# A four-part edit of a one-core mLSTM and mixture-of-experts step: stacked gate rows and an earlier gate product at the start, and the samples' tile ahead of the last prompt tile in the router

## The reference

```python
z = x @ w_in                       # q | k | v | o | 4+4 gate columns | pool input u | gate_A | gate_B
li, lf = gi + b_i, log_sigmoid(gf + b_f)
h, C, n, m = mlstm(q, k, v, li, lf, state_C, state_n, state_m)   # 4 heads x 256
y_a = (sigmoid(o) * head_norm(h)) @ w_proj_a
y_b = (causal_pool(u) @ w_pool * pool_scale) @ w_proj_b
x1 = layer_norm(ALPHA * x + (sigmoid(ga) * y_a + sigmoid(gb) * y_b) @ w_out)
probs = softmax(x1 @ w_router + b_router)          # 16 experts in 4 groups: best group, then its best two
y = layer_norm(ALPHA * x1 + sum over the two of weight * (silu(x1 @ w_gate[e]) * (x1 @ w_up[e])) @ w_down[e])
```

## Time and profile before

| what | value |
|---|---|
| median of 3 runs | 920.99 us |
| the runs | 921.68, 920.99, 919.57 us |
| the profiled execution | 921.98 us, of which its span is 920.6 us |
| mean granted clock of PE | 0.982 of full speed |
| busy: PE, DVE, ACT, POOL | 884.5, 587.3, 391.3, 87.2 us |

### The profile page before, as it was taken

One profiled execution on the slowest core, in us unless ns is written; L12 is line 12 of the kernel. 1 busy time (PEld: TensorE's weight loads), 2 busy tenths in 40 slices (PEclk: granted clock), 3 DMA queues, 4 the chain that ended last, 5 costly groups with the idle time before them and its releaser, 6 DMA issues.

```text
span 920.6 us, 14525 instructions
## 1 busy us (share of the span) xinstructions
PE 884.5 (96%) x6007; PEld 787.5 (86%) x6007; DVE 587.3 (64%) x825; ACT 391.3 (43%) x410; POOL 87.2 (9%) x88
## 2 busy tenths in 40 slices
PE   6999999999999999999999999999999999999975
PEld 6998888988889999999999996878888788778841
DVE  3735554745575371233233447899999999999946
ACT  4422132211432332322223104677777677777712
POOL 3000000000000001000101011301110011110043
PEclk8999999999999999999999998999999999999987
DMA  9784083483816042321322915799999999999657
GB/s 300 231 318 110 30 262 105 134 256 102 281 58 206 1 152 92 92 89 54 98 82 99 384 50 213 279 376 381 414 389 392 384 413 401 380 414 379 257 165 173
DMA packets 82212, 207.08 MB, mean 225 GB/s; under 512 B 4222, under 2 KB 57174, under 8 KB 69225
## 3 DMA queue, kind: packets, MB, share of 16 engines
q1 hardware_dynamic: 74184, 177.30, 53.4%
q0 software_dynamic: 7968, 28.93, 9.2%
HBM read 174.68 MB, written 33.76 MB: 226 GB/s over the span
## 4 chain that ended last, share of the span: by engine, by line
PE 74%; DVE 16%; issue 4%; ACT 3%; DMA 2%; POOL 0%; SPq 0%; DVEq 0%; ACTq 0%
PE psum L452 21%; PE psum L454 20%; PE psum L453 20%; DVE split_lo L1467 7%; PE psum L1908 2%; DVE last_lo L1467 2%; PE psum L1918 2%; PE psum L2131 2%; PE psum L1947 1%; DVE xgl L1627 1%; DMA xn<-in_x_prompt_dram 1%; ACT split_hi L1001 1%; PE psum L1933 1%; DVE hs L1636 1%; DVE gs L1633 1%
## 5 line engine op out<-in xcount | busy, mean ns | idle before, releaser
L452 PE MATMUL psum<-x_hi,split_lo 128*128 128x272 f32 x704 | 208.8, 297 | 2.0 <-DVE pbl L1430 1.2
L454 PE MATMUL psum<-x_hi,split_hi 128*128 128x272 f32 x704 | 202.3, 287 | 0.0
L453 PE MATMUL psum<-x_lo,split_hi 128*128 128x272 f32 x704 | 202.1, 287 | 0.0
L1467 DVE TENSOR_TENSOR split_lo<-raw,split_hi 128x2048 fp32r<-128x2048 f32 x72 | 163.3, 2286 | 7.9 <-ACT split_hi L1001 6.9
L1001 ACT CAST split_hi<-raw 128x2048 fp32r<-128x2048 f32 x72 | 137.5, 1912 | 44.1 <-PE psum L454 44.0
L447 DVE TENSOR_TENSOR split_lo<-raw,split_hi 128x2048 fp32r<-128x2048 f32 x35 | 80.0, 2289 | 115.0 <-ACT split_hi L428 114.9
L452 PEld LDWEIGHTS psum<-x_hi,split_lo 128*128 128x128 f32 x704 | 132.6, 188 | 7.3 <-issue 2.7
L453 PEld LDWEIGHTS psum<-x_lo,split_hi 128*128 128x128 f32 x704 | 132.7, 189 | 1.4 <-issue 1.0
L454 PEld LDWEIGHTS psum<-x_hi,split_hi 128*128 128x128 f32 x704 | 132.6, 188 | 0.0
L452 PE MATMUL psum<-split_hi,xgl 128*128 128x512 f32 x192 | 76.3, 398 | 1.3 <-DVE xgl L1627 1.2
L454 PE MATMUL psum<-split_hi,xgh 128*128 128x512 f32 x192 | 74.9, 390 | 0.0
(11 more groups left out here) (383 smaller groups left out, 1753.3 us busy)
## 6 DMA issues: line engine op xcount, KB each, us to landing
raw<-in_w_e_gate_dram SPq DMA_DIRECT2D x32, 1024.0 KB, 8.7
raw<-in_w_e_up_dram SPq DMA_DIRECT2D x32, 1024.0 KB, 8.6
raw<-in_w_e_down_dram SPq DMA_DIRECT2D x32, 1024.0 KB, 8.2
raw<-in_w_in_dram SPq DMA_DIRECT2D x26, 1024.0 KB, 5.6
cb<-in_state_C_dram SPq DMA_DIRECT2D x8, 1024.0 KB, 7.5
out_dram<-cb SPq DMA_DIRECT2D x8, 1024.0 KB, 5.8
y_slots<-ys POOLq DMA_DIRECT2D x15, 512.0 KB, 8.0
kv<-kv_rows SPq DMA_DIRECT2D x4, 1028.0 KB, 8.0
```

The source lines that it names most:

```text
L452: nc.tensor.matmul(out, a_lo, b_hi, start=first, stop=False)
L453: nc.tensor.matmul(out, a_hi, b_lo, start=False, stop=False)
L454: return nc.tensor.matmul(out, a_hi, b_hi, start=False, stop=last)
L1467: v.tensor_tensor(lo, raw2[:, n % MOE_SLOTS, :], hi.bitcast(F32), ALU.subtract).then_inc(w_lo, 1)
```

## The change

There are four parts.

1. **Stacked gate rows.** `g_r`, `em` and `w_r` become rows 0 to 3, 32 to 35 and 64 to 67 of one tile `turn3` of 68 partitions and 640 columns, cleared by DVE at the start. ACT copies the sample columns of all three in one instruction. PE makes 5 transposes of 68 rows in place of 15 of 4 rows. DVE picks the columns out of the wider result. `rep4` is gone.
2. **G earlier.** The samples' x tile is transposed into banks 2 and 3 and waits for `x_lo` of tile 1. G's first half (tokens 0 to 271) waits for three low parts, only its second for all five.
3. **POOL's small loads.** `nn` is issued after `nm_rows`; `gain`, `pscale`, `brt` and `wr` after `bm`.
4. **The router.** The order is 0, 1, 2, 4, 3. The last tile, now number 3, goes by columns: DVE adds columns 256 to 767 and takes the first half's statistics before the last 256 columns of the product exist; its last norm step, PE's transposes, ACT's copy and the logits are made in halves of 512 features, with four new semaphores. ACT makes only one expert split before this copy. SP loads `kv` ahead of tile 3's store alone.

```diff
+ROW_ORDER = (0, 1, 2, PT, 3)
...
+TURNED = 64 + H
...
+    g_r, em, w_r = (turn3[32 * q:32 * q + H, 0:N] for q in range(3))
...
-        return psum[:, 2 * (i % 4):2 * (i % 4) + 2, :]
+        b = i if i < PT else 1
+        return psum[:, 2 * b:2 * b + 2, :]
...
-            for i in range(NT):
-                if i == 3:
+            for n, i in enumerate(ROW_ORDER):
+                if n == NT - 1:
                     load_keys_values()
-                sp.wait_ge(x1_ok, i + 1)
+                sp.wait_ge(x1_ok, n + 1)
...
-            pl.dma_start(nn[:], state_n[0].rearrange("b h d -> (b h) d")).then_inc(nn_in, 16)
+        pl.wait_ge(cst_in, 16)
+
+
+        pl.wait_ge(nm_ok, 1)
+        pl.dma_start(nm_rows, nm[:]).then_inc(nm_out, 16)
+        pl.dma_start(nn[:], state_n[0].rearrange("b h d -> (b h) d")).then_inc(nn_in, 16)
+        pl.wait_ge(nm_out, 16)
+        pl.dma_start(bm[:].rearrange("p h n -> p (h n)"), nm_rows.rearrange("h n -> (h n)").partition_broadcast(P)
+                     ).then_inc(bm_in, 16)
+        with nc.allow_non_contiguous_dma(reason="small parameters"):
             pl.dma_start(gain[:], hn_gain[0].rearrange("h (c p) -> p (h c)", p=P)).then_inc(par_in, 16)
...
-        for q, row in enumerate((g_r, em, w_r)):
-            last = nc.scalar.copy(rep4[:, q, :].rearrange("p (g n) -> p g n", g=4),
-                                  row[:, SEQ:N].unsqueeze(1).to_broadcast([H, 4, NS]))
-        last.then_inc(em_ok, 1)
+        nc.scalar.copy(turn3[:, N:].rearrange("p (g n) -> p g n", g=3),
+                       turn3[:, SEQ:N].unsqueeze(1).to_broadcast([TURNED, 3, NS])).then_inc(em_ok, 1)
...
+            ac.wait_ge(xq_done, 1)
+            nc.scalar.copy(x1t[n % 2][:, 0:4, 0:r], src[:, 0:4, :]).then_inc(xq_ok, 1)
             ac.wait_ge(z_done, j + 1)
+            nc.scalar.copy(x1t[n % 2][:, 4:8, 0:r], src[:, 4:8, :]).then_inc(z_free[j % 2], 1)
...
-        for n in range(2):
-            expert_hi(n, z_done, Z["T", NT - 1] + 1)
+        expert_hi(0, z_done, Z["T", ROW_ORDER[-1]] + 1)
         evac_x1t(NT - 1)
+        expert_hi(1, z_done, Z["T", ROW_ORDER[-1]] + 1)
...
+        v.memset(turn3[:], 0.0)
...
+            ve_.wait_ge(tq_done, 1)
+            step(v.scalar_tensor_tensor(x1[:, i, 256:768], x1[:, i, 256:768], ALPHA, rest[:, 0:512], ALU.mult, ALU.add))
+            v.bn_stats(lst[:, i, 0, :], x1[:, i, 0:512])
+            ve_.wait_ge(z_done, j + 1)
+            v.scalar_tensor_tensor(x1[:, i, 768:DM], x1[:, i, 768:DM], ALPHA, rest[:, 512:768], ALU.mult, ALU.add
+                                   ).then_inc(z_free[j % 2], 1)
+            z_evacuated(ve_, j)
+            step(v.bn_stats(lst[:, i, 1, :], x1[:, i, 512:DM]))
...
+            if n == NT - 1:
+                v.scalar_tensor_tensor(x1[:, i, 0:512], x1[:, i, 0:512], hrs[:, i:i + 1], lnb[:, 0:512], ALU.mult, ALU.add
+                                       ).then_inc(xh_ok, 1)
+                v.scalar_tensor_tensor(x1[:, i, 512:DM], x1[:, i, 512:DM], hrs[:, i:i + 1], lnb[:, 512:DM], ALU.mult,
+                                       ALU.add).then_inc(x1_ok, 1)
...
-            if i == 4:
-                pe.wait_ge(x_lo_ok, 1)
+            if i == PT:
+                pe.wait_ge(x_lo_ok, 2)
...
-        pe.wait_ge(x_lo_ok, NT)
+        pe.wait_ge(x_lo_ok, 3)
...
+            if a == 1:
+                pe.wait_ge(x_lo_ok, NT)
...
-        for q, row in enumerate((g_r, em, w_r)):
-            for i in range(NT):
-                at = (q * NT + i) * H
-                src = row[:, i * P:i * P + P] if i < PT else rep4[:, q, :]
-                last = nc.tensor.transpose(narrow(T_COL)[:, at:at + H], src, ident[0:H, 0:H])
+        for i in range(NT):
+            last = nc.tensor.transpose(narrow(T_COL)[:, 96 * i:96 * i + TURNED], turn3[:, i * P:i * P + P],
+                                       ident[0:TURNED, 0:TURNED])
```

More of the change, by code:

```diff
@@ L74, in _wide_order @@
     order += [("WO", 0)]
-    for i in range(NT):
-        order += [("T", i)] + ([("XT", i - 1)] if i else [])
-    order += [("XT", NT - 1)]
+    for n in range(NT):
+        order += [("T", ROW_ORDER[n])] + ([("XT", ROW_ORDER[n - 1])] if n else [])
+    order += [("XT", ROW_ORDER[-1])]
     return {unit: i for i, unit in enumerate(order)}
@@ L1491, in _, with last_rows @@
         ve_.wait_ge(ln_in, 32)
-        for i in range(NT):
+        def last_rows(i):
+            j = Z["T", i]
+            rest = wide(j).rearrange("p b n -> p (b n)")
+            ve_.wait_ge(tq_done, 1)
[6 more added lines that the diff above has]
+            step(v.bn_stats(lst[:, i, 1, :], x1[:, i, 512:DM]))
+            step(v.bn_aggr(hmv[:, i, :], lst[:, i].rearrange("p q s -> p (q s)")))
+            v.tensor_scalar(hve[:, i:i + 1], hmv[:, i, 1:2], EPS, None, ALU.add).then_inc(lv_ok, 1)
@@ L1503, in _ @@
-            last.then_inc(z_free[j % 2], 1)
-            z_evacuated(ve_, J_WO)
-            z_evacuated(ve_, j)
-            row_stats(i, lv_ok)
+            if n == NT - 1:
+                last_rows(i)
+            else:
+                ve_.wait_ge(z_done, j + 1)
+                if i < PT:
+                    last = v.scalar_tensor_tensor(x1[0:r, i, 256:DM], x1[0:r, i, 256:DM], ALPHA,
+                                                  wide(j).rearrange("p b n -> p (b n)")[0:r, 0:DM - 256], ALU.mult,
+                                                  ALU.add)
+                else:
+                    for q in range(4):
+                        cols = slice(256 * q, 256 * q + 256)
+                        last = v.scalar_tensor_tensor(x1[0:r, i, cols], x1[0:r, i, cols], ALPHA,
+                                                      wide(j)[q * NS:(q + 1) * NS, 0, 0:256], ALU.mult, ALU.add)
+                last.then_inc(z_free[j % 2], 1)
+                z_evacuated(ve_, J_WO)
+                z_evacuated(ve_, j)
+                row_stats(i, lv_ok)
@@ L2068, in rest_of_rows @@
                 last = out_rows(i, q, wide(j).rearrange("p b (q n) -> p (b q) n", q=2)[:, q - 1, :])
+                if i == ROW_ORDER[-1] and q == 2:
+                    last.then_inc(tq_done, 1)
             last.then_inc(z_done, 1)
@@ L2089, in x1_columns, with logits_in @@
             for k in range(KT):
+                if n == NT - 1 and k == 4:
+                    last.then_inc(xq_done, 1)
+                    pe.wait_ge(x1_ok, n + 1)
                 last = nc.tensor.transpose(out[:, k, 0:r], x1[0:r, i, whole(k)], ident[0:r, 0:r])
             last.then_inc(z_done, 1)
-        def logits_in(i):
+        def logits_in(n):
+            i = ROW_ORDER[n]
             r = ROWS[i]
-            z_evacuated(pe, Z["XT", i])
+            if n == NT - 1:
+                pe.wait_ge(xq_ok, 1)
+            else:
+                z_evacuated(pe, Z["XT", i])
             for k in range(KT):
-                last = mm(narrow(T_LOGIT)[0:r, i * NE:(i + 1) * NE], x1t[i % 2][:, k, 0:r], wr[:, k, :],
+                if n == NT - 1 and k == 4:
+                    z_evacuated(pe, Z["XT", i])
+                last = mm(narrow(T_LOGIT)[0:r, i * NE:(i + 1) * NE], x1t[n % 2][:, k, 0:r], wr[:, k, :],
                           start=k == 0, stop=k == KT - 1)
@@ L2103, in _ @@
         rest_of_rows(0)
-        for i in range(1, NT):
-            if i < PT:
-                rest_of_rows(i)
+        for n in range(1, NT):
+            if ROW_ORDER[n] < PT:
+                rest_of_rows(ROW_ORDER[n])
             else:
                 sample_rows_of_out()
-            if i >= 2:
-                logits_in(i - 2)
-            x1_columns(i - 1)
+            if n >= 2:
+                logits_in(n - 2)
+            x1_columns(n - 1)
         logits_in(NT - 2)
```

68 lines of the change are left out of this document (31 added, 37 removed).

## The result

The changed kernel took 915.28 us (median of four runs, 914.45 to 915.86) against 920.89 before (919.57 to 921.68): ratio 0.9942, 95% interval 0.9927 to 0.9957, a gain of 5.6 us. The forecast was 916.8, a gain of 4.2, within 913.8 to 919.3. The profiled execution took 915.86 us with a span of 913.7 us and a mean granted clock of 0.986 (before 921.98, 920.6 and 0.982).

A forecast was written before the change was run, and what follows sets the result against it. PE bounds the kernel, with 74% of what ended last (DVE 16%). Gains of 2.8 (G earlier), 0.4 (stacked rows), 0 (loads) and 1.0 (router) sum to 4.2 us: 920.99 to 916.8 us, range 913.8 to 919.3.

The forecast's parts named there:

- five of 68 rows lie between 0.34 and 0.68 us; I take 0.6: Gate rows' transposes after K: five stacked ones take 0.6 us against 1.02 for fifteen; gain 0.4 us, bounds 0.3 to 0.7.
- Rival B: Clock dip after K (1.7 us) goes; G at full clock gives 0.9, router 0.7 more: 913.5 us; chance 0.13.
- within 3.6 us of uninterrupted matmuls: At G: clock returns after 3.5 us, 16 slow matmuls, then 32 fast; G ends at 20.6, gain 2.8 us.
- upper bound of 3.7: At G: clock never low, G ends at 19.15, but Q waits for its chunk's low part until 19.71; gain 3.7 us.
- Nothing above depends on it: POOL's loads at the start: five fewer transfers can only bring x tiles and first chunks earlier; gain 0.
- the middle between 0 and 1.9: Router: gain between 0 and 1.9 us, depending on PE's clock at the last tile; 1.0 us taken.
- The sign that was named for a wrong forecast: Router: PE's clock low across the last tile's logits, 0.2 us a pass.
- rival A: Only the start pays: clock falls before the last tile's logits, or the store's landing takes the router's gain; 917.8 us; chance 0.2.
- the forecast's 575.5: Router's end: tile 3's store, issued at 565.4, lands at about 575.5 us if it ends with the queue's bytes.
- Rival D: Slower: tile 3's store lands late and delays POOL's first gather; at 20 us it costs 3.7, 924.7 us; chance 0.04.
- C: The start doesn't arrive: G's clock rises when it does now (gain 1.1), router gives nothing; 919.6 us; chance 0.10.
- E: Change doesn't do what it says: G starts with the gate weights' low part, at 13.01; later only if DVE's order delays it; no separate chance.

The follow-up runs named there:

- e5: Kernel before with part 1 alone (stacked gate rows): 918.96 us, ratio 0.9979.
- e3: Kernel before with part 2 alone (G's first half waits for three low parts): 917.96 us, ratio 0.9969.
- e7: Kernel before with 14 extra unused transposes on PE in its wait ahead of G, G's start condition unchanged: 918.30 us, ratio 0.9974.
- e6: Kernel before with parts 2 and 3, without the stacked rows: 916.99 us, ratio 0.9963.
- e1: Kernel before with part 4 alone (the router's order and the halves): 920.69 us, ratio 1.0004.
- e10: Changed kernel with 8 filler transposes on PE in the router (2, 3 and 3): 915.70 us, ratio 0.9946.
- e8: Changed kernel with 20 filler transposes on PE in the router (8, 6 and 6): 915.06 us, ratio 0.9938.
- e12: Changed kernel with the 20 router fillers of e8 and 10 more in PE's wait behind the twelfth expert's second product: 913.67 us, ratio 0.9929.
- e4: Kernel before with part 3 alone (POOL's small loads later): 920.48 us, ratio 0.9993.

## Why the prediction was right, and where it was not

**The sum** of 4.2 us was 1.4 short of 5.6. The interval of the measured gain reaches from 4.0 to 6.7 us, so the total alone would not fault it; the parts do. The mechanism, an earlier G and nothing that waits in its place, was right; three terms were mis-sized. That the sum is as near as it is owes something to luck, since part 4's missing 1.0 us stands against part 1's surplus of 1.5.

**Part 1, too small, and its pricing failed.** The step "five of 68 rows lie between 0.34 and 0.68 us; I take 0.6" was wrong: they took 0.31 on the chain, 0.062 each against 0.068 for those of 4 rows, and the gain up to the copied columns was 0.7, the upper bound. Between 4 and 68 rows the size did not matter. The Trainium skill, "TensorE: Matmul & The Clock Gate", section "LDWEIGHTS (loading the stationary operand)", had the 0.34 us and the gain of 0.7; by that rule, the trace agrees, and I had set it aside for a difference between a light transpose at 4 rows and one of full rows whose other dimension differed too. Rival B's second mechanism, the fall after K that goes away, came true on top in e5's profile, 1.4 us of the 1.7 that the earlier trace rows priced. I gave all of B 0.13.

**Part 2, right at the end, in part by luck.** Forecast 2.8, alone 2.9 (e3). G's start was 13.25 for 13.05. The step that took the clock's return "within 3.6 us of uninterrupted matmuls", 16 slow matmuls and then 32 fast, failed: all 48 ran at 2.4 GHz. G's result came 4.26 us earlier, above the upper bound of 3.7, since that bound kept the first chunk's low part at 19.71 us, and it was there at 18.04; without that wait the same sum gives 23.4 - 19.15 = 4.25. In e3, where the chunk comes as before, it was at 20.14 and PE did wait, as the bound has it. e7 shows the share of the clock: 2.51 us at G's end with G's start left as it was. The luck is in the 2.9: e3's profile is 3.8 us ahead at G's copy and 4.8 at the values', and only the slower runs with a lower clock bring its median back to the forecast's 2.8.

**Part 3, forecast 0, an omission.** "Nothing above depends on it" is the step that failed: the first chunk did, once G ended before its low part. Alone it is not told from 0 (0.9993, interval up to 1.0005), beside part 2 the columns come 1.1 us earlier in e6's profile than in e3's. The waits it adds cost nothing: `nn` landed 3.1 us after issue, `gain`, `pscale` and `brt` 6.9 to 7.7 us after theirs, all before 47; DVE began the split behind them 0.52 us after it was free, under the cover of the earlier trace rows.

**Part 4, forecast 1.0, worth 0** (e1: 1.0004, interval from 0.9993, so 0.6 us of gain at most). The steps up to the last tile's transposes held: they start 4.1 us after the last product, forecast 3.8. "1.7 us, at full clock" was right too: e10 shows 1.68. What failed is the choice of the middle between 0 and 1.9. It had the argument for 0 beside it, that the tile of 128 tokens is now the one made at low clock: the transposes took 1.97 for the 1.1 assumed, the logits 3.42 for some 2. The sign that was named for a wrong forecast, about 0.2 us a pass across the last tile's logits, was there: 3.42 / 16 = 0.21. That is rival A's mechanism in the router, with rival B's at the start. The idle gaps, fewer after the change, did not make the low clock "come later or last less": it began at 557.2 us, 2.7 us after the last product, where it was 566.6 and 5.7 us before. What a held clock would have made of part 4 in the time of the kernel stays open, as e8, e10 and e12 leave it.

**SP's store** landed as forecast. The issue came at 559.21, 9.9 us before it was in, and SP's timeline of the changed kernel goes on at

```profile
569.09 0.33 SPq L622 DMA_DIRECT2D lng<-in_ln_g_dram  x1
```

that is 14.6 us after the last product, where the earlier trace rows had 15.0; the forecast's 575.5 was 14.6. Rival D's 20 us are not near. Rivals C and E did not occur.

## What to carry to other kernels

Price a change in the stretches of small work by both levels of PE's clock, and look for the next wait of PE from which the clock could fall: a fall that is removed is worth as much as the work (e7), and in the profiles of e8 and e10 one came 240 us later, where none was before, and cost 1.6 us. Hold the granted clock of every run against that of the profiled one before a median is explained by a profile (e3, e7, e10). Where an order is changed so that the last work is larger, ask at which clock it will run. When a start moves forward by several us, list again what arrives around the new end, the loads of other queues with it (e3, e6).

## What the runs showed of the hardware

- G had 1.2 GHz in the profiles of before, e4 and e5 and 2.4 in e1's, with the same code for it and 2.00 to 2.08 us of idle time ahead of it: the fall is not fixed by the program, and medians of many runs are needed. Within one kernel the time goes with the granted clock: e3's twelve runs reach from 915.35 us at 0.988 to 921.49 at 0.984 and 920.55 at 0.981. The nine runs of the changed kernel lie closer together (913.94 to 915.86, clock 0.986 to 0.988), but a steady clock is no promise of a steady time: e12's six, at 0.991 and 0.992, reach from 912.77 to 916.68.
- Fourteen transposes of no use in a 2 us wait kept 2.4 GHz for the matmuls behind them, worth 2.5 us at G's end in that profile.
- Transposes of 4 and of 68 rows cost the same, 0.068 and 0.062 us; those of 128 rows 0.136.
- The first weight chunk landed 1.2 to 1.9 us earlier (e4 against before, e6 against e3, by the start of ACT's split that waits for it) when five loads were moved behind it that hold only 110 KB together (`nn` 32, `gain` 4, `pscale` 2, `brt` 8, `wr` 64).
